# Decoder trunk step: conditions and first conditioning columns reordered, first product group cut into half-depth products

## The chip, the cores and the metric

The kernel runs on one core of a Trainium2 chip. The metric is the device time of one execution in microseconds (us).

## What is computed

A two-layer decoder trunk works on 288 rows (256 of a prompt, 32 of samples) of 2048 features. Only the start of layer 0 matters here:

```python
m = jax.nn.silu(c) @ w + b                 # c: 9 condition rows, w: 2048 x 6144
shift, scale, gate = jnp.split(m[:, None, :], 3, axis=-1)
h = rmsnorm(x, norm_g[layer]) * (1.0 + scale) + shift
... = jnp.split(h @ w_in, idx, axis=-1)    # w_in: 2048 x 7168
```

So no product with `w_in` can start before the shift and the scale of at least some features are there, and these are themselves a product of the condition rows with a 2048-deep matrix of 50 MB per layer.

## The kernel before

Features lie on the partitions in 16 blocks of 128, `k` = 0 to 15. Each product in `w_in` is made three times for precision: the weight is split into a high and a low part (`WHI` by ScalarE in `hi`, L293; `WLO` by VectorE in `lo`, L298), and so is the input (`HH`, `HL`), and `product` issues three matmuls (L304, L307, L308).

**Weights** come in chunks of 512 KB, numbered `i`, into four slots `WRAW[i % 4]`: four blocks `k` deep and 256 columns wide. The load of chunk `i` waits until `lo(i - 4)` has read its slot. A step `i` of the first 48 (`part_products`) has 24 matmuls with one chunk. Steps 0 to 11 multiply blocks 0 to 3, steps 12 to 23 blocks 4 to 7 and so on; VectorE takes each step's partial sum out of PSUM (`part_out`: a copy, L674, in the first group, an addition, L678, in the later ones). Three pairs of PSUM banks take turns, so step `i` waits for the sum of step `i - 3`.

**Conditioning columns** come in units `a` of 4 MB, each 512 columns over the full depth of 2048, in eight loads into the buffer `XR`, which holds one unit. `ada_sum` (L390, 16 matmuls that the trace shows as 32) sums a unit quarter by quarter and frees each quarter (`x_used`); `ada_copy` (ScalarE, L398), `ada_turn` (L403) and `ada_home` (VectorE, L412, L415) bring it into `ADA`. Unit 0 holds the shift of blocks 0 to 3, unit 1 their scale; units 2 and 3 the same for blocks 4 to 7. With both, `scale4` and `modulate4` make the input of four blocks, and `lo_part` (L447) its low part.

**Order.** Each engine runs its own list in order and waits on semaphores in it. SyncE's list holds all these loads: unit 0, chunk 0, unit 1, chunks 1 to 3, unit 2, chunks 4 to 10, unit 3, chunks 11 to 15, unit 4 and so on. A load of unit `a` waits for the sum of unit `a - 1`. The loop of the first 48 steps is, per step `i`:

```python
part_products(pe, i)                       # TensorE; then a sum if i in SUM_AT, a turn if i in TURN_AT
hi(act, i + 4)                             # ScalarE; then ada_copy, modulate4
part_out(dve, i); lo(dve, i + 4)           # VectorE; then ada_home, scale4, lo_part
```

Before the loop, units 0 and 1 are summed and the input rows turned (`x_turn`, L498) on TensorE, in that order of arrival: rows, conditions, unit 0, rows, unit 1. VectorE scales the turned rows (`x_scaled`, L537) and builds a mask (`own_mask`, L579 to L585).

## Time and profile before

| | |
|---|---|
| median of 3 runs | 1283.02 us (1279.35 to 1283.18) |
| the profiled execution, its own time | 1283.61 us |
| its span in the profile | 1281.9 us |
| TensorE busy | 1197.0 us, 93% |
| chain that ended last | TensorE 83% of the span |

The span leaves 1.7 us of the profiled execution's own time outside. TensorE's idle time is what the time can be shortened by, and most of it lies in the first 75 us.

### The profile page before, as it was taken

The numbers are of one execution on the slowest core, as the hardware profiler recorded it, in microseconds if no ns is written. First come the engines' busy times: TensorE is split into PE (matmuls) and PEld (weight loads), VectorE is DVE, ScalarE is ACT, GpSimd is POOL, SyncE is SP. The second block draws the span as 40 slices with busy tenths as digits, with TensorE's granted clock in tenths as the row PEclk, the third lists the DMA queues.
The fourth block names the chain that finished last, engine by engine and source line by source line (L and its number), as shares of the span: only waits on it lengthen the run. The fifth ranks groups of instructions, "written<-read, shape, count | busy, mean of one in ns | idle before, by whom it ended". The sixth has DMA issues, their size and how long they took to land.

```text
span 1281.9 us, 23762 instructions
## 1 busy us (share of the span) xinstructions
PE 1197.0 (93%) x9394; PEld 1064.2 (83%) x9394; DVE 714.5 (56%) x1343; ACT 564.6 (44%) x715; POOL 335.9 (26%) x195
## 2 busy tenths in 40 slices
PE   5799999999999899999999995999999999989995
PEld 2589797978888778788889885999998999989995
DVE  2745556554544546534355446399999993583112
ACT  3323433333343444422243235466666664473442
POOL 1000000000000001000000002565676668486771
PEclk9899999999999999999999998999999999999998
DMA  9999899999887767999999993384766445353432
GB/s 302 329 315 339 279 333 313 379 360 331 295 300 256 270 225 270 300 354 320 348 369 341 309 323 117 97 280 158 254 211 217 154 141 179 101 165 132 163 117 90
DMA packets 236276, 324.89 MB, mean 253 GB/s; under 512 B 12366, under 2 KB 152462, under 8 KB 235246
## 3 DMA queue, kind: packets, MB, share of 16 engines
...
## 4 chain that ended last, share of the span: by engine, by line
PE 83%; DVE 6%; DMA 4%; issue 2%; ACT 2%; SPq 2%; POOL 0%; ACTq 0%; DVEq 0%; POOLq 0%
PE PS L304 21%; PE PS L308 20%; PE PS L307 20%; PE PS L390 6%; PE PS L973 4%; PE PS L1001 3%; PE PS L1210 2%; DMA XR<-in_ada_w 2%; SPq L377 2%; DVE ACTS L1820 1%; DMA WRAW<-in_ab_w_out 1%; DMA ACTS<-in_x_sample 1%; DVE WLO L298 1%; PE PS L403 1%; ACT WHI L293 1%
## 5 line engine op out<-in xcount | busy, mean ns | idle before, releaser
L304 PE MATMUL PS<-HH,WHI 128*128 128x288 f32 x2176 | 665.9, 306 | 32.0 <-DVE HL L447 20.6
L308 PE MATMUL PS<-HH,WLO 128*128 128x288 f32 x2176 | 646.0, 297 | 0.0
L307 PE MATMUL PS<-HL,WHI 128*128 128x288 f32 x2176 | 645.9, 297 | 0.0
L304 PEld LDWEIGHTS PS<-HH,WHI 128*128 128x128 f32 x2176 | 413.1, 190 | 55.0 <-issue 41.7
L293 ACT ACTIVATE WHI<-WRAW 128x1024 fp32r<-128x1024 f32 x272 | 283.9, 1055 | 371.1 <-PE PS L308 320.5
L307 PEld LDWEIGHTS PS<-HL,WHI 128*128 128x128 f32 x2176 | 413.7, 190 | 0.1
L308 PEld LDWEIGHTS PS<-HH,WLO 128*128 128x128 f32 x2176 | 412.9, 190 | 0.0
L298 POOL TENSOR_TENSOR WLO<-WRAW,WHI 128x1024 fp32r<-128x1024 f32 x128 | 308.1, 2424 | 232.6 <-ACT WHI L293 232.6
L298 DVE TENSOR_TENSOR WLO<-WRAW,WHI 128x1024 fp32r<-128x1024 f32 x144 | 175.9, 1224 | 162.9 <-ACT WHI L293 161.6
L1662 DVE SCALAR_TENSOR_TENSOR PS<-ACTS,CWT,PS 128x288 f32<-128x288 f32 x448 | 192.5, 514 | 0.0
L1638 ACT ACTIVATE ACTS<-ACTS 128x1088 f32<-128x1088 f32 x32 | 70.3, 2197 | 61.2 <-DVE ACTS L1660 34.8
L390 PE MATMUL PS<-XR,CT 128*32 128x512 f32 x768 | 89.6, 606 | 4.3 <-DMA XR<-in_ada_w 3.9
L986 DVE COPY ACTS<-PS 128x512 f32<-128x512 f32 x64 | 44.1, 689 | 78.8 <-PE PS L973 78.1
L973 PE MATMUL PS<-IDENT,XR 128*128 128x128 f32 x512 | 77.7, 274 | 5.1 <-DVE ACTS L986 3.5
L984 ACT ACTIVATE ACTS<-PS 128x512 f32<-128x512 f32 x64 | 38.3, 598 | 81.8 <-PE PS L973 79.8
L973 PEld LDWEIGHTS PS<-IDENT,XR 128*128 128x128 f32 x512 | 60.8, 140 | 11.9 <-issue 4.9
L390 PEld LDWEIGHTS PS<-XR,CT 128*32 128x32 f32 x768 | 22.6, 111 | 53.5 <-issue 45.8
L1428 POOL DMA_DIRECT2D ACTS<-in_a_ws x1 | 0.9, 945 | 230.3 <-PE PS L1001 230.3
L430 DVE TENSOR_TENSOR PS<-PS,ADA 128x64 f32<-128x64 f32 x24 | 5.5, 228 | 88.5 <-PE PS L308 88.5
L678 DVE TENSOR_TENSOR ACTS<-PS,ACTS 128x576 f32<-128x576 f32 x36 | 27.2, 756 | 45.3 <-PE PS L308 45.3
L636 POOL IOTA ACTS<- 128x128 f32 x1 | 0.2, 242 | 193.0 <-DVE HL L447 193.0
L1001 PE MATMUL PS<-ACTS 128*32 128x256 f32 x512 | 32.1, 392 | 6.5 <-DVE ACTS L986 3.8
...
## 6 DMA issues: line engine op xcount, KB each, us to landing
XR<-in_ada_w SPq DMA_DIRECT2D x192, 512.0 KB, 8.5
WRAW<-in_ab_w_in SPq DMA_DIRECT2D x112, 512.0 KB, 7.4
WRAW<-in_c_w_in SPq DMA_DIRECT2D x96, 512.0 KB, 3.8
XR<-in_cache_b_k SPq DMA_DIRECT2D x128, 256.0 KB, 5.0
XR<-in_cache_b_v SPq DMA_DIRECT2D x128, 256.0 KB, 5.5
WRAW<-in_ab_w_out SPq DMA_DIRECT2D x32, 512.0 KB, 10.0
WRAW<-in_c_w_out SPq DMA_DIRECT2D x32, 512.0 KB, 3.2
...
```

What stands on the lines that cost most here:

```text
L293: act.activation(WHI[:, i % 4], WRAW[:, i % 4], ACT.Copy).then_inc(w_hi, 1)
L298: eng.tensor_tensor(WLO[:, c], WRAW[:, c], WHI[:, c].bitcast(F32), ALU.subtract).then_inc(w_lo[c], 1)
L304: first = pe.matmul(out, whi, HH[:, k, :], start=start, stop=False)
L307: pe.matmul(out, whi, HL[:, k, :], start=False, stop=False)
L308: return pe.matmul(out, wlo, HH[:, k, :], start=False, stop=stop)
L390: last = pe.matmul(PS[32 * kk:32 * kk + 32, bank, :], CT[:, 4 * c + kk, :], XR[:, c, kk * 512:(kk + 1) * 512], start=c == 0, stop=c == 3)
L973: last = pe.transpose(PS[:, (M2, M3)[g % 2], (2 * h2 + t) * P:(2 * h2 + t + 1) * P], XR[:, c, at:at + P], IDENT[:])
L984: eng.activation(dst, PS[:, M2, :], ACT.Copy).then_inc(kt_a, 1)
L986: eng.tensor_copy(dst, PS[:, M3, :]).then_inc(kt_d, 1)
L1001: last = pe.matmul(PS[32 * j:32 * j + 32, M0, 0:BLOCK], QM[:, j, h, :], KT[:, hh % 2, j, h2, :], start=h == 0, stop=h == HEADS - 1)
L1638: act.activation(EX[:, lo:hi, 0:64], src, ACT.Copy)
L1662: ins = dve.scalar_tensor_tensor(dst, src, tap, dst, ALU.mult, ALU.add)
```

## The change

Condition rows are loaded and turned first, the input rows after them; the rows' transposes lie between the quarters of unit 0's sum. Units 0 and 1 are now shift and scale together, of blocks 0 and 1 (unit 0) and of blocks 2 and 3 (unit 1), 256 columns each. Only unit 0 is summed before the loop; unit 1 after step 3, unit 2 after step 7, unit 3 after step 11. The first twelve chunks are two blocks deep and 512 columns wide, so steps 0 to 5 need blocks 0 and 1 alone and steps 6 to 11 blocks 2 and 3. Each of these steps makes two half steps with a PSUM bank pair each, and `first_out` takes both sums out: for steps 0 to 5 the first by ScalarE and the second by VectorE, for steps 6 to 11 both by VectorE. The low parts of chunks 0 to 3 go to GpSimd. The turning of the convolution's weights (31 small transposes) moves from after step 4 to after step 3.

```diff
 
+            if i < 12:
+                return win_v, 2 * (i // 6), 3072 + 512 * (i % 6)
             if i < 48:
                 return win_v, 4 * (i // 12), 256 * (12 + i % 12)
...
             c, (view, k, col) = i % 4, w_src(i)
             if i >= 4:
                 sp.wait_ge(w_lo[c], i // 4)
-            sp.dma_start(WRAW[:, c], view[:, k:k + 4, col:col + 256]).then_inc(w_raw[c], 16)
+            if i < 12:
+                sp.dma_start(WRAW[:, c].rearrange("p a b -> p (a b)").rearrange("p (k n) -> p k n", k=2),
+                             view[:, k:k + 2, col:col + 512]).then_inc(w_raw[c], 16)
+            else:
+                sp.dma_start(WRAW[:, c], view[:, k:k + 4, col:col + 256]).then_inc(w_raw[c], 16)
...
                 k = 4 * c + 2 * half
+                if a < 2:
+                    t = half
+                    sp.dma_start(XR[:, c].rearrange("p (k t n) -> p k t n", k=4, t=2)[:, :, t],
+                                 ada_v[0, :, 4 * c:4 * c + 4, 2048 * t + 256 * a:2048 * t + 256 * a + 256]).then_inc(x_rdy[c], 16)
+                    continue
...
+            if a < 2:
+                for t in range(2):
+                    dst = ADA[:, 16 * t + 2 * a:16 * t + 2 * a + 2, :]
+                    src = PS[:, M1, 256 * t:256 * t + 256].rearrange("p (m j r) -> p m r j", m=2, j=4)[:, :, 0:NC9, :]
+                    last = dve.tensor_reduce(dst, src, AX.X, ALU.add)
+                last.then_inc(ada_part, 1)
+                dve.wait_ge(ada_part, a + 1)
+                for t in range(2):
...
             ada_copy(act, 0, 0, M0)
             hi(act, 0)
+            hi(act, 1)
+            modulate(act, 0, 2, 1)
             act.wait_ge(xt_tr, KC)
             act.wait_ge(s_setup_pe, 2)
             act.dma_start(CWROW.rearrange("k (w p) -> k w p", p=P),
                           c_conv_w[0].rearrange("w (k p) -> k w p", p=P)).then_inc(s_cw, 16)
-            ada_copy(act, 1, 1, M0)
-            modulate4(act, 0)
-            for i in range(1, 4):
-                hi(act, i)
+            hi(act, 2)
+            hi(act, 3)
...
+            def between(c):
+                if c == 0:
+                    for t in range(3):
+                        pe.wait_ge(s_rows[t], 16)
+                    for k in range(2):
+                        x_turn(pe, k)
+                elif c == 1:
+                    for k in range(2, 6):
+                        x_turn(pe, k)
+                elif c == 2:
+                    pe.wait_ge(s_vec, 8 * 16)
+                    pe.transpose(PS[:, M2, 0:112], VROWS1, IDENT[0:112, 0:112])
+                    pe.transpose(PS[:, M2, 112:208], VROWS2, IDENT[0:96, 0:96]).then_inc(s_setup_pe, 1)
+                    for k in range(6, 11):
+                        x_turn(pe, k)
+
+            ada_sum(pe, 0, 0, M0, between)
             pe.wait_ge(x_diag, 1)
             for t, rows in ((0, P), (1, P), (2, NS * DS)):
                 last = pe.matmul(PS[:, M3, t * P:t * P + rows], ONES[0:rows, :], DIAG[0:rows, t * P:t * P + rows],
                                  start=True, stop=True)
             last.then_inc(x_rb, 1)
-            ada_sum(pe, 1, 1, M0)
-            ada_turn(pe, 1)
+            x_turn(pe, 11)
+            ada_turn(pe, 0)
+            for k in range(12, KC):
+                x_turn(pe, k)
...
         def start_dve(dve):
+            dve.memset(CROW, 0.0).then_inc(s_cz, 1)
+            dve.wait_ge(s_setup_pe, 1)
+            dve.tensor_copy(CT[:], PS[:, M3, :].rearrange("p (k c) -> p k c", c=32)).then_inc(s_setup_cp, 1)
             for k in range(4):
                 x_copy(dve, k)
-            dve.wait_ge(s_setup_pe, 1)
-            dve.tensor_copy(CT[:], PS[:, M3, :].rearrange("p (k c) -> p k c", c=32)).then_inc(s_setup_cp, 1)
...
+            dve.wait_ge(s_setup_cp, 2)
             ada_home(dve, 0)
+            scale(dve, 0, 2, 1, 1)
+            for k in range(12, KC):
+                x_copy(dve, k)
...
+            for k in range(2):
+                lo_part(dve, HF, k, k, k)
...
+            for i in range(4):
+                lo(pool, i)
             pool.wait_ge(s_hl, KC)
...
-        SUM_AT = {3: 2, 8: 3, 13: 4, 19: 5, 25: 6, 31: 7, 37: 8, 41: 9, 45: 10}
-        TURN_AT = {4: 2, 8: 3, 14: 4, 20: 5, 26: 6, 32: 7, 38: 8, 42: 9, 46: 10}
+        SUM_AT = {3: 1, 7: 2, 11: 3, 13: 4, 19: 5, 25: 6, 31: 7, 37: 8, 41: 9, 45: 10}
+        TURN_AT = {4: 1, 8: 2, 11: 3, 14: 4, 20: 5, 26: 6, 32: 7, 38: 8, 42: 9, 46: 10}
...
+        def first_products(pe, i):
+
+            pe.wait_ge(w_lo[i % 4], i // 4 + 1)
+            for half in range(2):
+                h = 2 * i + half
+                if h == 2:
+                    pe.wait_ge(s_seed_cp, 1)
+                if 3 <= h < 15:
+                    pe.wait_ge((acc_pa, acc_pd)[(h - 3) % 2], (h - 3) // 2 + 1)
+                elif h >= 15:
+                    pe.wait_ge(acc_free, h - 14)
+                for kk in range(2):
+                    k = 2 * (i // 6) + kk
+                    if i % 6 == 0:
+                        pe.wait_ge(s_hl, k + 1)
+                    for n in range(2):
+                        last = product(pe, i, 2 * kk + half, n, k, PART_SETS[h % 3], kk == 0, kk == 1)
+            last.then_inc(w_used, 1)
+
+        def first_out(eng, i, half):
+
+            j, banks = 2 * (i % 6) + half, PART_SETS[(2 * i + half) % 3]
+            eng.wait_ge(w_used, i + 1)
+            dst = A(2 * j * R, 2 * R).rearrange("p (c r) -> p c r", r=R)
+            src = PS[:, banks[0]:banks[0] + 2, 0:R]
+            if i < 6 and half == 0:
+                eng.activation(dst, src, ACT.Copy).then_inc(acc_pa, 1)
+            elif i < 6:
+                eng.tensor_copy(dst, src).then_inc(acc_pd, 1)
+            else:
+                eng.wait_ge((acc_pa, acc_pd)[half], i - 5)
+                eng.tensor_tensor(dst, src, dst, ALU.add).then_inc(acc_free, 1)
...
         def qkv_pe(pe):
             for i in range(NQKV):
                 part_products(pe, i)
+                if i == 3:
+                    pe.wait_ge(s_cw, 16)
+                    pe.wait_ge(ada_done, 1)
+                    for w in range(CW):
+                        last = pe.transpose(PS[:, M1, w * KC:(w + 1) * KC], CWROW[:, w * P:(w + 1) * P], IDENT[0:KC, 0:KC])
+                    last.then_inc(s_cwt, 1)
+                if i == 4:
...
                 hi(act, i + 4)
                 if i in SUM_AT:
                     ada_copy(act, SUM_AT[i], SUM_AT[i], M0)
-                if i in (8, 20, 32):
-                    modulate4(act, i // PAIRS_QKV + 1)
+                if i < 6:
+                    first_out(act, i, 0)
+                if i == 4:
+                    modulate(act, 2, 2, 2)
+                if i in (11, 20, 32):
+                    modulate(act, 4 * (i // PAIRS_QKV) + 4, 4, i // PAIRS_QKV + 3)
...
-                part_out(dve, i)
+                if kg:
+                    part_out(dve, i)
+                else:
+                    if i >= 6:
+                        first_out(dve, i, 0)
+                    first_out(dve, i, 1)
                 lo(dve, i + 4)
...
                 if i in TURN_AT:
                     ada_home(dve, TURN_AT[i])
-                    if i in (8, 20, 32):
-                        scale4(dve, kg + 1)
-                if kg < 3 and 9 <= j <= 10:
+                if i == 4:
+                    scale(dve, 2, 2, 2, 2)
+                    for k in (2, 3):
+                        lo_part(dve, HF, k, k, k)
+                if i in (11, 20, 32):
+                    scale(dve, 4 * kg + 4, 4, 2 * kg + 4, kg + 3)
+                if i == 11:
+                    for k in range(4, 8):
+                        lo_part(dve, HF, k, k, k)
...
             load_ada4(sp, 0, 0)
-            w_load(sp, 0)
-            load_ada4(sp, 1, 1)
-            i = 1
-            for a, upto in ((2, 4), (3, 11), (4, 16), (5, 21), (6, 27), (7, 33), (8, 39), (9, 45), (10, 49), (11, 53),
+            i = 0
+            for a, upto in ((1, 4), (2, 8), (3, 12), (4, 16), (5, 21), (6, 27), (7, 33), (8, 39), (9, 45), (10, 49), (11, 53),
```

**SyncE, the loads after unit 0** (`XR` is the buffer of the conditioning units, `WRAW` that of the chunks). Before:

```order
L377 DMA XR<-in_ada_w 128x2x512
L287 DMA WRAW<-in_ab_w_in 128x4x256 [waits w_lo0]
L287 DMA WRAW<-in_ab_w_in 128x4x256 [waits w_lo1]
L287 DMA WRAW<-in_ab_w_in 128x4x256 [waits w_lo2]
L287 DMA WRAW<-in_ab_w_in 128x4x256 [waits w_lo3]
L287 DMA WRAW<-in_ab_w_in 128x4x256 [waits w_lo0]
L287 DMA WRAW<-in_ab_w_in 128x4x256 [waits w_lo1]
L287 DMA WRAW<-in_ab_w_in 128x4x256 [waits w_lo2]
L377 DMA XR<-in_ada_w 128x2x512 [waits x_used0]
```

These are chunks 4 to 10 between the last load of unit 2 and the first of unit 3. Now, between the last load of unit 2 and the first of unit 3:

```order
L390 DMA XR<-in_ada_w 128x2x512
L292 DMA WRAW<-in_ab_w_in 128x2x512 [waits w_lo0]
L292 DMA WRAW<-in_ab_w_in 128x2x512 [waits w_lo1]
L292 DMA WRAW<-in_ab_w_in 128x2x512 [waits w_lo2]
L292 DMA WRAW<-in_ab_w_in 128x2x512 [waits w_lo3]
L390 DMA XR<-in_ada_w 128x2x512 [waits x_used0]
```

Now four chunks, 8 to 11, lie between them; chunk 8 stands behind unit 2 and chunk 12 behind unit 3.

**ScalarE, the loop's steps 3 and 4** (L301 is `hi`, L413 `ada_copy`, L738 `first_out`, L646 and L649 `modulate`). Before, with `hi` at L293 and `ada_copy` at L398:

```order
L293 ACTIVATE WHI<-WRAW 128x1024 [waits w_used,w_raw3]
L398 ACTIVATE SCR<-PS 128x512 [waits ada_turned,x_used3]
L293 ACTIVATE WHI<-WRAW 128x1024 [waits w_used,w_raw0]
L293 ACTIVATE WHI<-WRAW 128x1024 [waits w_used,w_raw1]
L293 ACTIVATE WHI<-WRAW 128x1024 [waits w_used,w_raw2]
```

Now:

```order
L301 ACTIVATE WHI<-WRAW 128x1024 [waits w_used,w_raw3]
L413 ACTIVATE SCR<-PS 128x512 [waits ada_turned,x_used3]
L738 ACTIVATE ACTS<-PS 128x576 [waits w_used]
L301 ACTIVATE WHI<-WRAW 128x1024 [waits w_used,w_raw0]
L738 ACTIVATE ACTS<-PS 128x576 [waits w_used]
L646 ACTIVATE ACTS<-ACTS,ADA 128x256 [waits x_times_factor,scale_ready]
L649 ACTIVATE HH<-ACTS 128x288 [waits rows_normalised,act_chain]
```

ScalarE now takes sums out of PSUM behind each `hi`: the L301 that waits for `w_raw0` is `hi(8)`, and the sum of step 4's first half stands behind it.

**TensorE, from the end of step 3 to step 5** (L762 are the 31 transposes, L403 the sum, L312 opens a product). Now:

```order
L762 MATMUL PS<-IDENT,ACTS 128x16 [waits ada_done,conv_weights_loaded]
L762 MATMUL PS<-IDENT,ACTS 128x16 x30
L403 MATMUL PS<-XR,CT 32x512 [waits x_rdy0,ada_done]
...
L312 MATMUL PS<-HH,WHI 128x288 [waits first_sums_by_dve,w_lo0]
...
L312 MATMUL PS<-HH,WHI 128x288 [waits first_sums_by_act]
...
L312 MATMUL PS<-HH,WHI 128x288 [waits first_sums_by_dve,w_lo1]
...
L312 MATMUL PS<-HH,WHI 128x288 [waits first_sums_by_act]
```

The transposes and a sum of a unit now stand between steps 3 and 4. Every second half step waits for a sum taken out by ScalarE, three half steps earlier.

## Rows read from the trace of the kernel before

**Rows 1.** The page: TensorE's busy tenths in 40 slices; GpSimd's low parts.

```profile
PE   5799999999999899999999995999999999989995
...
L298 POOL TENSOR_TENSOR WLO<-WRAW,WHI 128x1024 fp32r<-128x1024 f32 x128 | 308.1, 2424 | 232.6 <-ACT WHI L293 232.6
```

**Rows 2.** Windows of the front: length, busy us, clock, DMA share, GB/s.

```profile
46.00:58.00 12.00, 11.16 (x72) 10.86 (x72) 9.94 (x19) 5.20 (x9) 0.00 (x0) 0.88 1.07 375
72.00:76.00 4.00, 3.43 (x15) 3.44 (x16) 2.72 (x5) 0.00 (x0) 0.00 (x0) 0.59 1.05 402
80.00:150.00 70.00, 69.14 (x534) 60.46 (x532) 38.41 (x55) 28.27 (x37) 0.00 (x0) 1.00 0.93 316
```

**Rows 3.** Timeline of the first 27 us: start, length, engine, line.

```profile
8.26 1.28 ACT L472 ACT_TABLE_LOAD   x1 [8.26 <-issue]
15.25 3.48 PE L498 MATMUL PS<-IDENT,ACTS 128*128 128x128 f32 x12 [15.25 <-DMA ACTS<-in_x_sample]
18.55 1.89 PE L510 MATMUL PS<-IDENT,ACTS 32*128 32x32 f32 x16
21.22 5.47 PE L390 MATMUL PS<-XR,CT 128*32 128x512 f32 x32 [0.24 <-DVE CT L543]
26.62 6.59 PE L498 MATMUL PS<-IDENT,ACTS 128*128 128x128 f32 x36
```

**Rows 4.** Timeline: `ada_copy` after unit 1's sum, and the first product.

```profile
41.44 0.60 ACT L398 ACTIVATE SCR<-PS 128x512 f32<-128x512 f32 x1 [13.13 <-PE PS L390]
46.05 0.58 PE L304 MATMUL PS<-HH,WHI 128*128 128x288 f32 x1 [2.85 <-DVE HL L447]
```

**Rows 5.** The chain that ended last: the sums of units 4 and 5.

```profile
107.99 3.57 PE PS L390 x32
131.31 3.57 PE PS L390 x32
```

**Rows 6.** Timeline of ScalarE: `hi` of chunks 4, 15, 16 and 27.

```profile
57.90 1.06 ACT L293 ACTIVATE WHI<-WRAW 128x1024 fp32r<-128x1024 f32 x1 [6.74 <-DMA WRAW<-in_ab_w_in]
101.72 1.06 ACT L293 ACTIVATE WHI<-WRAW 128x1024 fp32r<-128x1024 f32 x1 [2.12 <-PE PS L308]
104.90 1.06 ACT L293 ACTIVATE WHI<-WRAW 128x1024 fp32r<-128x1024 f32 x1 [2.12 <-PE PS L308]
148.87 1.06 ACT L293 ACTIVATE WHI<-WRAW 128x1024 fp32r<-128x1024 f32 x1 [1.30 <-DMA WRAW<-in_ab_w_in]
```

**Rows 7.** Timeline of SyncE: unit 6's loads and chunk 27 behind them.

```profile
132.37 4.86 SPq L377 DMA_DIRECT2D XR<-in_ada_w  x8
137.27 0.89 SPq L287 DMA_DIRECT2D WRAW<-in_ab_w_in  x1
```

**Rows 8.** DMA issues to landing: at 60.24, at 137.27, at 136.3 to 137.2 us.

```profile
WRAW<-in_ab_w_in SPq DMA_DIRECT2D x1, 512.0 KB, 3.7
WRAW<-in_ab_w_in SPq DMA_DIRECT2D x1, 512.0 KB, 11.6
XR<-in_ada_w SPq DMA_DIRECT2D x2, 512.0 KB, 9.9
```

**Rows 9.** Groups by line and form, first 250 us: busy, mean ns.

```profile
L298 DVE TENSOR_TENSOR WLO<-WRAW,WHI 128x1024 fp32r<-128x1024 f32 x51 | 62.2, 1223 | 24.1 <-ACT WHI L293 23.9
L293 ACT ACTIVATE WHI<-WRAW 128x1024 fp32r<-128x1024 f32 x51 | 53.5, 1057 | 100.3 <-PE PS L308 84.6 <-DMA WRAW<-in_ab_w_in 15.7
L674 DVE COPY ACTS<-PS 128x576 f32<-128x576 f32 x12 | 9.0, 754 | 6.5 <-PE PS L308 6.5
L537 DVE TENSOR_TENSOR ACTS<-XT,SCR 128x1152 f32<-128x1152 f32 x4 | 5.2, 1353 | 0.0
L691 PE MATMUL PS<-IDENT,ACTS 16*128 16x16 f32 x31 | 2.1, 209 | 0.0
```

**Rows 10.** DMA packets of 124 to 128 us and of 138 to 142 us.

```profile
DMA packets 1318, 1.32 MB, mean 330 GB/s; under 512 B 45, under 2 KB 1317, under 8 KB 1317
DMA packets 822, 1.59 MB, mean 396 GB/s; under 512 B 48, under 2 KB 48, under 8 KB 822
```

More of the change, by code:

```diff
@@ L382, in load_ada4, with ada_sum @@
                 load_ada(sp, x, a, c)
-        def ada_sum(pe, x, a, bank):
+        def ada_sum(pe, x, a, bank, between=None):
             if a:
@@ L392, in ada_sum @@
                 last.then_inc(x_used[c], 1)
+                if between is not None:
+                    between(c)
         def ada_copy(act, x, a, bank):
@@ L503, in start_pe @@
             pe.wait_ge(s_ident, 3)
-            for t in range(3):
-                pe.wait_ge(s_rows[t], 16)
-            for k in range(4):
-                x_turn(pe, k)
             pe.wait_ge(s_silu, 1)
@@ L548, in start_dve @@
             dve.reciprocal(RT[:, 0:3], RT[:, 0:3]).then_inc(s_stat, 1)
-            for k in range(4, KC):
+            for k in range(4, 8):
                 x_copy(dve, k)
@@ L555, in start_dve @@
             last.then_inc(x_diag, 1)
+            dve.wait_ge(s_setup_pe, 2)
+            dve.tensor_copy(VT[:], PS[:, M2, 0:208]).then_inc(s_setup_cp, 1)
+            for k in range(8, 11):
+                x_copy(dve, k)
+            dve.wait_ge(x_rb, 1)
+            link(dve, "dve", dve.tensor_copy(RB, PS[:, M3, 0:R]))
+            dve.wait_ge(xt_cp, 4)
+            x_scaled(dve, 0)
+            x_copy(dve, 11)
+            dve.wait_ge(s_setup_cp, 2)
             ada_home(dve, 0)
+            scale(dve, 0, 2, 1, 1)
+            for k in range(12, KC):
+                x_copy(dve, k)
             dve.wait_ge(s_setup_pe, 3)
             dve.tensor_copy(QROW, PS[:, M2, 0:1])
[L559 to L561 removed]
+            dve.tensor_copy(SLROW, PS[:, M2, 32:33]).then_inc(s_seed_cp, 1)
+            for k in range(2):
+                lo_part(dve, HF, k, k, k)
             dve.wait_ge(xt_cp, KC)
[L563 to L570 removed]
             for kg in range(1, 4):
                 x_scaled(dve, kg)
+            dve.wait_ge(s_seed_cp, 1)
             own_mask(dve)
@@ L686, in qkv_pe @@
                     ada_turn(pe, TURN_AT[i])
-                if i == 4:
-                    pe.wait_ge(s_cw, 16)
-                    pe.wait_ge(acc_free, 3)
-                    for w in range(CW):
-                        last = pe.transpose(PS[:, M3, w * KC:(w + 1) * KC], CWROW[:, w * P:(w + 1) * P], IDENT[0:KC, 0:KC])
-                    last.then_inc(s_cwt, 1)
-                    pe.wait_ge(s_setup_cp, 4)
                 if i >= 45:
```

86 lines of the change are left out of this document (37 added, 49 removed).

## The prediction

> **What bounds the kernel now.** I read the page first: TensorE's slices are full except the first two, the seam at slice 25 and the end [rows 1]. So TensorE bounds the kernel, and any us by which its work stands earlier or later in the front is a us of the total. The windows show that the front ends early: from 80 us on TensorE is busy 69.14 of 70 us at full clock, while DMA moves 316 GB/s of the 396 that it can reach [rows 2, 10], so it has some room. Therefore one number decides: when TensorE begins the sum of unit 4 (after step 13). Before, this is at 107.99 us [rows 5]. From there on the lists of all engines are the same in both kernels, and the next sum follows 23.3 us later [rows 5].
>
> **Work of TensorE up to that sum.** A step of 24 matmuls takes 3.18 us at full clock (104.90 - 101.72) [rows 6], a sum 3.6 [rows 5], the 31 transposes 2.1 [rows 9], a turn 0.6. Before, from the first product at 46.05 [rows 4]: 14 steps 44.5, two sums 7.2, two turns 1.2, transposes 2.1, together 55.0, so 101.1; the other 6.9 us to 107.99 are waits and half clock. The half clock (1.2 of 2.4 GHz) shows at the first product, after a pause of 2.85 us [rows 4], and again after the transposes: 72 matmuls in 11.16 us instead of 9.6, and clock 0.59 in 72 to 76 [rows 2]; each start after a pause costs about 1.5 us.
>
> **Start after the change.** ScalarE's list of loads still holds its table load until about 8.3 + 0.4 us (one more issue ahead of it), and silu ends near 11.9 [rows 3]. The 16 turns of the conditions (1.9) and their copy (0.7) give 14.6, and the first quarter of unit 0's sum (5.47 / 4 = 1.4) ends at 16. The rows came at 15.25 [rows 3]; their first load was issued at 0.8 and now stands behind the zeroing of the condition rows, about 2.4 us later, so I take 18.5 (bounds 17 and 20: only shifted, or slowed by sharing with unit 0 as well). Then TensorE owes 11 row turns (0.87 each slow, 3.48 / 4; 0.55 fast, 6.59 / 12 [rows 3]; five slow, six fast, 7.7), three quarters of the sum (3.6) and the vectors (0.8): unit 0 is summed at 30.6. From there to the first product the new list on VectorE decides: factors 1.0 on TensorE, copy 0.5, scaling 1.35 [rows 9], a row copy 0.5, `ada_home` 0.9, scale and sample rows 1.0, four row copies 2.0, the seeds 0.3, `lo_part` 0.5: 8.0 us, so 38.6. Apart from the scaling these are estimates, small instructions of 0.2 to 0.7 us as the 4.6 us chain from copy to first product holds some ten of [rows 4]. This is 7.4 us earlier than 46.05. Bounds 36 and 40. GpSimd's low parts (2.42 us each [rows 1], twice the 1.22 of VectorE [rows 9]) are ready at 35 and 37.5 for the first two steps and cost nothing there.
>
> **What the new order adds before unit 4's sum.** A third sum and turn, 4.2 us, since unit 1 moves behind the first product. The 12 extra takings out of PSUM are 0.75 us each [rows 9]. On VectorE they fit in a step (2 x 0.75 + 1.22 = 2.7 of 3.18). On ScalarE the half-step sum stands behind `hi`: 1.06 + 0.7 + handshakes = 1.95 against the 1.6 us that TensorE can run on, so 0.35 in each of steps 0 to 2, 1.05 together. So without other waits: 38.6 + 55.0 + 4.2 + 1.05 + 1.5 (half clock at the start) = 100.4, 7.6 us better than before. Step 3 then ends at 54.0 and the sum of unit 1 begins at 56.1.
>
> **First wait: chunk 8 behind unit 2.** Unit 2 can load only as unit 1's sum frees `XR`. The same pattern is measured at unit 6: sum at 131.31, first issue at 132.37, the last load of the unit lands at 147.1 (137.2 + 9.9), and the chunk behind it at 148.9 (137.27 + 11.6), where `hi` waits for it [rows 5 to 8]. Chunk 4 behind unit 2 held `hi` for 6.74 us in the old front as well [rows 6]. So a chunk behind a unit lands 17.5 us after the start of the sum: chunk 8 at 73.6. Before, such a chunk had 7 chunks of lead at unit 3; now every unit up to 3 is followed by the chunk that is needed four steps on. `hi(8)` stands in ScalarE's list ahead of the sum of step 4's first half, and the second half of step 5 needs those banks. With `hi` 1.1, the copy 0.7 and handshakes this half step starts at 56.1 + 19.5 = 75.6; TensorE is there at 56.1 + 3.6 + 3.2 + 0.6 + 1.6 = 65.1. Wait 10.5 us. Behind `hi(8)` VectorE also holds `lo(8)`, `ada_home(1)`, `scale`, and then ScalarE `modulate`: step 6 starts 0.6 us late on its own, a half clock costs 1.5. The end of step 7 comes 10.7 us after this half step: the sum of unit 2 begins at 86.3.
>
> **Second wait: chunk 12 behind unit 3.** It lands at 86.3 + 17.5 = 103.8. Now both sums are VectorE's, and `lo(12)` and `ada_home(2)` stand ahead of the sums of step 9: 103.8 + 1.1 + 1.3 + 0.5 + 0.8 = 107.5 for the second half of step 10. TensorE is there at 86.3 + 12.2 = 98.5 (sum, steps 8 and 9, turn, half a step). Wait 9.0 us and again 1.4 of half clock. Step 11 ends 6.3 us later, 113.8.
>
> **Third wait: blocks 4 to 7.** Before, they were made ready under steps 9 to 11. Now unit 3 is summed right ahead of step 12, and TensorE waits for copy, turn, home, scale, modulate and low part, bounded by what it was before the first product: 4.6 us from 41.44 to 46.05 [rows 4], of which the slow turn was 0.5; I take 4.2, and 0.7 since the four blocks come one by one. 113.8 + 3.6 + 4.2 = 121.6; steps 12 and 13 take 7.1: unit 4's sum begins at 128.7. Its own data, asked for at 114.9, land by 129.7, before its last quarter needs them.
>
> **The sum.** 128.7 - 108.0 = +20.7 us, made against the profiled execution: 1283.6 + 20.7 = 1304.3; the median is 0.6 us lower, so 1303.7.
>
> **Where the price is open.** The lag of 17.5 us counts about twice. Its lower end is a lone chunk's 3.7 us and eight loads at 396 GB/s (8 x 1.32), with the 1.1 to the first issue 15.4 [rows 8, 10]: 4 us less in all. Packets: units 0 and 1 go from 2 KB to 1 KB rows and the first twelve chunks the other way; windows of such packets ran at 330 and 396 GB/s [rows 10], but the first was not short of data. A slow unit 0 (4.2 MB, 2.1 us more) is hidden behind the rows, chunks 0 to 7 land well ahead of use.
>
> The Trainium skill, "DMA: Bandwidth & Descriptors", section "Anatomy of one DMA", fits a DMA from GpSimd's queue to about 2.0 us and its bytes at 436 GB/s. By it the nine loads would take 2.0 + 4.72 / 0.436 = 12.8 us as one stream, where rows 7 and 8 show 16.5; with it each wait would be 3.7 us shorter and the sum 1296. This trace disagrees: these are SyncE's loads, issued as the sum frees quarters.
>
> **Rivals.**
> (a) The forecast: both waits form. 1298 to 1310, chance 0.58.
> (b) The stream is faster than under unit 6, because SyncE's list and the queue are empty when the sum begins. The lag is then between 15.4 and 13.0 (4.72 MB at 396 GB/s and the 1.1 to the first issue [rows 7, 10]); at 14, each wait is 3.5 us smaller: 1303.7 - 7 = 1296.7, chance 0.12. Against it: the issues are paced by the sum's quarters here too. The skill's fit named above would lead to this case.
> (c) Only one wait forms, since chunk 12's lag is taken up by VectorE's margin of one and a half steps: 10.4 us less, 1293, chance 0.08. Against it: the margin is already in the 98.5.
> (d) No wait: loads and chunks overlap so that chunk 8 lands within 7 us of the sum's start (that is the point where it decides), say because the two queues' data arrive in another order. Then 20.7 - 10.5 - 0.6 - 1.5 - 9.0 - 1.4 = -2.3 us: 1281. With the first product at 36 instead of 38.6 this is -5, faster by over 0.3%. For it speaks only the earlier start of 7.4 us; against it 4.7 MB at 396 GB/s. Chance 0.10, of which 0.05 faster.
> (e) More is lost: rows landing at 20, the clock lower for longer after each of three pauses, or chunk 16 behind unit 4 (lands at 131.3, held in VectorE's list ahead of step 14's sum) reaching TensorE: 5 to 10 us more, 1309 to 1314, chance 0.12.
>
> **How the numbers follow.** A measurement tells 0.3% (3.9 us) from no change. Faster is half of (d), 0.05; the same is the other half, 0.05; slower the rest, 0.90. The range 1293 to 1312 leaves out (d) and the ends of (c) and (e), under 0.2; the likeliest case alone has 1298 to 1310.
>
> **What the profile would show.** Right: first product near 38.6; `hi` (L301) waiting some 10 us for DMA near 73 and again near 103; a TensorE wait of about 10 us in the middle of step 5 whose releaser is ScalarE's L738, one of about 9 in step 10 released by VectorE's L743; 4 us ahead of step 12 released by L475; the fourth unit's sum (L403) near 128.7; DMA slices below half near 50 us and 80 us. Wrong: chunk 8 landing before 66 us, or the unit 4 sum before 108.

## The result, and the profile after

| | before | after |
|---|---|---|
| median | 1283.02 us (1279.35 to 1283.18) | 1313.13 us (1309.52 to 1315.33, 4 runs) |
| the profiled execution | 1283.61 us, span 1281.9 | 1309.52 us, span 1307.2 |
| sum of unit 4 starts | 107.99 [rows 5] | 133.52 |

The changed kernel is slower: ratio 1.0239, 95% interval 1.0208 to 1.027, some 30 us. The two profiled executions differ by 25.9 us, and 25.5 of them (133.52 - 107.99) are there when the sum of unit 4 starts. So the front holds the loss, and what comes behind it runs as before.

The page of the changed kernel, TensorE's busy tenths in 40 slices, to be laid beside [rows 1]; the loss is in slices 3 and 4:

```profile
PE   5776999999999899999999988799999999998995
```

Its waits up to 134 us: engine, what it made, line, what it waited for; us in all, times, the longest.

```profile
ACT WHI L301 <- DMA WRAW<-in_ab_w_in: 34.9, 5, 12.9
...
PE PS L312 <- ACT ACTS L738: 9.7, 3, 9.3
...
PE PS L312 <- DVE HL L475: 8.9, 3, 5.9
...
PE PS L312 <- DVE ACTS L743: 8.5, 1, 8.5
...
PE PS L312 <- DVE ACTS L740: 2.2, 1, 2.2
```

Of TensorE's idle time behind the first product 9.3 us are released by `first_out` on ScalarE (L738) and 8.5 by `first_out` on VectorE (L743). Both engines wait in turn for `hi`, and `hi` waits 34.9 us for chunks. The timeline of TensorE places the waits between the sums (start, length, line, and the idle time before with its releaser):

```profile
39.91 0.58 PE L312 MATMUL PS<-HH,WHI 128*128 128x288 f32 x1 [5.87 <-DVE HL L475]
...
50.73 0.37 PE L312 MATMUL PS<-HH,WHI 128*128 128x288 f32 x1 [2.15 <-DVE ACTS L740]
...
59.72 5.34 PE L403 MATMUL PS<-XR,CT 128*32 128x512 f32 x32
...
79.79 0.61 PE L312 MATMUL PS<-HH,WHI 128*128 128x288 f32 x1 [9.32 <-ACT ACTS L738]
...
90.24 3.64 PE L403 MATMUL PS<-XR,CT 128*32 128x512 f32 x32
...
110.96 0.61 PE L312 MATMUL PS<-HH,WHI 128*128 128x288 f32 x1 [8.50 <-DVE ACTS L743]
...
117.74 3.64 PE L403 MATMUL PS<-XR,CT 128*32 128x512 f32 x32
...
125.60 0.58 PE L312 MATMUL PS<-HH,WHI 128*128 128x288 f32 x1 [2.85 <-DVE HL L475]
...
133.52 3.64 PE L403 MATMUL PS<-XR,CT 128*32 128x512 f32 x32
```

And ScalarE's, where `hi` of chunks 8 and 12 waits, to be laid beside [rows 6]:

```profile
78.14 1.06 ACT L301 ACTIVATE WHI<-WRAW 128x1024 fp32r<-128x1024 f32 x1 [11.88 <-DMA WRAW<-in_ab_w_in]
79.10 0.63 ACT L738 ACTIVATE ACTS<-PS 128x576 f32<-128x576 f32 x1
...
107.48 1.06 ACT L301 ACTIVATE WHI<-WRAW 128x1024 fp32r<-128x1024 f32 x1 [12.93 <-DMA WRAW<-in_ab_w_in]
```

Read the two together: unit 1's sum begins at 59.72, chunk 8 can be split at 78.14, 18.4 us later; the copy that stands behind `hi` in ScalarE's list ends at 79.7, and TensorE starts at 79.79. For unit 2 and chunk 12 it is 90.24 and 107.48, 17.2 us. Windows of the time before and inside these stretches (length; busy us of TensorE, its weight loads, VectorE, ScalarE, GpSimd; clock; DMA share; GB/s):

```profile
52.00:60.00 8.00, 7.84 (x76) 7.29 (x78) 5.31 (x6) 2.66 (x3) 0.00 (x0) 1.00 0.01 2
60.00:64.00 4.00, 4.00 (x24) 1.00 (x20) 0.76 (x2) 0.00 (x0) 0.00 (x0) 0.57 0.40 109
72.00:76.00 4.00, 0.00 (x0) 0.00 (x0) 0.00 (x0) 0.00 (x0) 0.00 (x0) 0.76 1.05 398
76.00:80.00 4.00, 0.21 (x1) 0.21 (x2) 0.77 (x1) 1.59 (x2) 0.00 (x0) 0.50 0.92 339
80.00:84.00 4.00, 3.82 (x15) 3.50 (x16) 2.69 (x12) 2.44 (x5) 0.00 (x0) 0.50 0.05 20
84.00:92.00 8.00, 8.00 (x67) 6.64 (x69) 6.04 (x9) 3.15 (x4) 0.00 (x0) 0.98 0.01 2
```

From 52 to 60 and from 84 to 92 us the DMA engines move 2 GB/s: the whole list of loads stands behind a unit whose buffer is in use. Then they run at 398 GB/s while no engine has work, and TensorE starts again at half clock.

### The profile page after: what moved, and what is told of

Same layout as the page of the kernel before. It is cut to its first block, busy times and chain, and to the rows that moved or that the text cites. A ratio compares the mean times of both kernels' runs of the same rounds, so it can differ in the third digit from the quotient of the medians.

```text
span 1307.2 us, 23801 instructions
## 1 busy us (share of the span) xinstructions
PE 1202.7 (92%) x9394; PEld 1067.7 (82%) x9394; DVE 723.5 (55%) x1354; ACT 568.1 (43%) x721; POOL 346.3 (26%) x198
## 3 DMA queue, kind: packets, MB, share of 16 engines
q1 hardware_dynamic: 234064, 312.78, 70.7%
## 4 chain that ended last, share of the span: by engine, by line
PE 81%; DVE 7%; DMA 5%; issue 3%; ACT 2%; SPq 2%; ACTq 0%; DVEq 0%
PE PS L312 20%; PE PS L316 20%; PE PS L315 20%; PE PS L403 6%; PE PS L1065 4%; PE PS L1093 2%; PE PS L1302 2%; SPq L390 2%; DMA WRAW<-in_ab_w_in 2%; DVE ACTS L1912 1%; DMA XR<-in_ada_w 1%; DMA ACTS<-in_x_sample 1%; DMA WRAW<-in_ab_w_out 1%; ACT WHI L301 1%; DVE WLO L306 1%
## 5 line engine op out<-in xcount | busy, mean ns | idle before, releaser
L312 PE MATMUL PS<-HH,WHI 128*128 128x288 f32 x2176 | 668.5, 307 | 55.4 <-DVE HL L475 26.6
L312 PEld LDWEIGHTS PS<-HH,WHI 128*128 128x128 f32 x2176 | 415.0, 191 | 80.3 <-issue 50.6
L301 ACT ACTIVATE WHI<-WRAW 128x1024 fp32r<-128x1024 f32 x272 | 284.0, 1056 | 393.9 <-PE PS L316 304.6
L306 POOL TENSOR_TENSOR WLO<-WRAW,WHI 128x1024 fp32r<-128x1024 f32 x132 | 320.4, 2444 | 262.7 <-ACT WHI L301 262.7
L306 DVE TENSOR_TENSOR WLO<-WRAW,WHI 128x1024 fp32r<-128x1024 f32 x140 | 171.2, 1224 | 183.4 <-ACT WHI L301 182.2
L403 PE MATMUL PS<-XR,CT 128*32 128x512 f32 x768 | 91.6, 615 | 2.5 <-DMA XR<-in_ada_w 1.6
L403 PEld LDWEIGHTS PS<-XR,CT 128*32 128x32 f32 x768 | 22.5, 111 | 49.5 <-issue 44.4
## 6 DMA issues: line engine op xcount, KB each, us to landing
WRAW<-in_ab_w_out SPq DMA_DIRECT2D x32, 512.0 KB, 10.1
```

Of the source, the lines that this page charges most:

```text
L301: act.activation(WHI[:, i % 4], WRAW[:, i % 4], ACT.Copy).then_inc(w_hi, 1)
L306: eng.tensor_tensor(WLO[:, c], WRAW[:, c], WHI[:, c].bitcast(F32), ALU.subtract).then_inc(w_lo[c], 1)
L312: first = pe.matmul(out, whi, HH[:, k, :], start=start, stop=False)
L403: last = pe.matmul(PS[32 * kk:32 * kk + 32, bank, :], CT[:, 4 * c + kk, :], XR[:, c, kk * 512:(kk + 1) * 512], start=c == 0, stop=c == 3)
```

## The experiments

Each was timed beside the kernel before on the same chip, with medians of before between 1281.46 and 1284.14 us. Interval: 95%, of the ratio to before.

| run | median us | ratio | interval |
|---|---|---|---|
| after, a second time | 1314.79 | 1.0242 | 1.0219 to 1.0265 |
| chunks 8 to 11 ahead of unit 2 | 1303.35 | 1.0159 | 1.0142 to 1.0176 |
| chunks 12 to 14 ahead of unit 3 | 1303.87 | 1.0165 | 1.0148 to 1.0182 |
| both | 1293.04 | 1.0087 | 1.0067 to 1.0106 |
| unit 2 summed after step 5 | 1304.71 | 1.0159 | 1.0133 to 1.0184 |
| ScalarE's sums ahead of `hi` | 1313.03 | 1.0245 | 1.0218 to 1.0272 |
| low parts on VectorE | 1311.65 | 1.0223 | 1.0202 to 1.0244 |
| unit 1 summed before the loop | 1294.41 | 1.0089 | 1.0066 to 1.0112 |
| the same, chunks 4, 5 ahead of unit 2 | 1292.11 | 1.0082 | 1.006 to 1.0104 |
| both, units 2 and 3 summed earlier | 1288.74 | 1.0045 | 1.0028 to 1.0062 |
| before, conditions first alone | 1285.14 | 1.0015 | 1.0 to 1.003 |
| reordered | 1280.56 | 1.000 | 0.9983 to 1.0016 |

**The two waits, one at a time.** Only SyncE's list is changed: which chunks are issued ahead of unit `a`.

```diff
-            for a, upto in ((1, 4), (2, 8), (3, 12), (4, 16),
+            for a, upto in ((1, 4), (2, 12), (3, 12), (4, 16),
```

> The changed kernel with one edit: SyncE loads chunks 8 to 11 ahead of unit 2 instead of behind it. Theory (chunk 8's lag behind unit 2 makes the first wait): the 9.3 us wait in step 5 goes, step 6 starts near 73 instead of 83.2 us, the second wait (8.5 us in step 10) stays; the time falls by 9 to 11 us against the changed kernel, to about 1303. Rival (the half steps with their sums behind each hi cost the time, whatever the loads do): less than 3 us.

```diff
-            for a, upto in ((1, 4), (2, 8), (3, 12), (4, 16),
+            for a, upto in ((1, 4), (2, 8), (3, 15), (4, 16),
```

> The changed kernel with one edit: chunks 12 to 14 are loaded ahead of unit 3, chunk 15 behind it. Theory (chunk 12's lag behind unit 3 makes the second wait): the 9.3 us wait in step 5 stays, the 8.5 us wait in step 10 goes, step 12 starts near 115 instead of 125.6; the time falls by 9 to 11 us, to about 1303. Rival (half steps): less than 3 us.

```diff
-            for a, upto in ((1, 4), (2, 8), (3, 12), (4, 16),
+            for a, upto in ((1, 4), (2, 12), (3, 15), (4, 16),
```

> Both edits: chunks 8 to 11 ahead of unit 2 and 12 to 14 ahead of unit 3. Theory: the gains add up, 19 to 22 us, to about 1292; the fourth unit's sum starts near 113 instead of 133.5; what is left above the kernel before is the wait ahead of step 12 and the slow start. Rival (the loads only move the wait to the next unit, since the DMA queue has no room): 10 us or less together.

Each takes its own wait away and leaves the other (8.74 us of the second and 8.39 us of the first). Their steps stand 3 to 6 us later than expected, since their first products begin at 44.7 to 45.2 instead of 39.91. The first is worth 9.8 us (1313.13 - 1303.35), the second 9.3, both together 20.1: they add up, and each is one wait with its half clock behind it. With both gone no wait of TensorE behind the first product is longer than 2.85 us, yet 10.5 us of loss remain (1293.04 against 1282.55). The two waits are two thirds of the loss, not all.

**The lag that starts at a sum.**

```diff
-        SUM_AT = {3: 1, 7: 2, 11: 3,
+        SUM_AT = {3: 1, 5: 2, 11: 3,
-        TURN_AT = {4: 1, 8: 2, 11: 3,
+        TURN_AT = {4: 1, 6: 2, 11: 3,
```

> The sum of unit 2 after step 5 instead of step 7, nothing else; the list of loads stays. Theory (a lag that runs from a unit's sum: chunk 12 stands behind unit 3, whose loads start as unit 2's sum frees the buffer): the sum starts near 83 us instead of 90.24, chunk 12 lands 17.2 us later near 100, the second half of step 10 could start at 83 + 20.7 = 103.7, and TensorE is there at 102.5, so the second wait falls from 8.5 to some 1.2 us and little half clock is left of it: median 1304 to 1307. The first wait stays at 9.3. Rival (the second wait is VectorE's own list, or chunk 12 comes at a time of its own): the wait stays at 8 to 9 us and the time at 1313.

Timelines of TensorE and ScalarE in this kernel:

```profile
87.53 4.19 PE L403 MATMUL PS<-XR,CT 128*32 128x512 f32 x32
...
106.21 1.06 ACT L301 ACTIVATE WHI<-WRAW 128x1024 fp32r<-128x1024 f32 x1 [6.31 <-DMA WRAW<-in_ab_w_in]
...
109.24 0.61 PE L312 MATMUL PS<-HH,WHI 128*128 128x288 f32 x1 [2.54 <-DVE ACTS L743]
```

Here the chunk came 18.7 us after the sum began, and the wait fell from 8.50 to 2.54 us (1.2 was expected, with a lag of 17.2). The time fell by 10.1 us beside the second look at the changed kernel on the same chip (1314.79). The profile shows about half of it: from the first product to the sum of unit 4 this kernel takes 88.2 us and the changed one 93.6. Its profiled execution, 1310.56 us, starts the first product at 44.64 and is the slowest of its five, so where the rest of the 10.1 us lies is not shown. Unit 2's columns are needed much later: their sum is early only because it lets chunk 12 in. The rival, a wait of VectorE's own, falls: TensorE still starts some 3 us behind the split of chunk 12 (3.0 here, 3.5 in the changed kernel).

**Does the order in ScalarE's list matter?**

```diff
+                if i < 6:
+                    first_out(act, i, 0)
                 hi(act, i + 4)
                 if i in SUM_AT:
                     ada_copy(act, SUM_AT[i], SUM_AT[i], M0)
-                if i < 6:
-                    first_out(act, i, 0)
```

> The changed kernel with ScalarE's sums of steps 0 to 5 ahead of hi in its list, so that none of them stands behind a chunk that is late. Theory (the chunk is what all wait for; the input of blocks 2 and 3 stands behind it too, on VectorE and ScalarE): the 9.3 us wait moves from step 5 to the start of step 6 and shrinks by the half step to about 7.7, so the time falls by 1 to 3 us, most of it from the half-step handshakes. Rival (the place of ScalarE's sums makes the wait): the wait goes, and 8 to 10 us with it.

The wait moved by half a step and did not shrink: 10.39 us, where 7.7 were expected and 9.32 were there before this edit; the gain of 1 to 3 us did not come. In this kernel's timeline of TensorE:

```profile
84.31 0.58 PE L312 MATMUL PS<-HH,WHI 128*128 128x288 f32 x1 [10.39 <-DVE HL L475]
```

Now the wait ends with blocks 2 and 3 (`HL`), whose scale on VectorE and modulation on ScalarE still stand behind chunk 8's parts. The late chunk is the cause, and the instruction that passes it on can be exchanged.

**GpSimd's low parts beside VectorE.** `lo` of chunks 0 to 3 is moved from GpSimd's list into VectorE's.

```diff
+            lo(dve, 0)
...
+            for i in range(1, 4):
+                lo(dve, i)
...
-            for i in range(4):
-                lo(pool, i)
```

> The changed kernel with the low parts of chunks 0 to 3 back on VectorE (chunk 0's ahead of the first input's low part, 1 to 3 behind the second's). Theory (a low part on GpSimd stops VectorE's instructions that need the same way into memory): the 2.20 us of the scale's first instruction falls to 0.2, the three scalings from 8.2 us together to about 4.0, the first product starts near 37.8 instead of 39.9, and the time falls by 2 to 4 us. Rival (these instructions are slow for another reason, such as DMA traffic): they stay slow, and 4.9 us more work on VectorE makes the kernel 3 to 6 us slower.

First VectorE and GpSimd in the changed kernel, then VectorE with the low parts moved:

```profile
32.80 0.36 DVE L429 TENSOR_REDUCE ADA<-PS 128x18 f32<-128x72 f32 x2
33.20 1.64 DVE L435 TENSOR_TENSOR ADA<-ADA,VT 128x18 f32<-128x18 f32 x2
34.88 2.20 DVE L634 TENSOR_SCALAR ADA<-ADA 128x18 f32<-128x18 f32 x1
...
40.05 8.27 DVE L574 TENSOR_TENSOR ACTS<-XT,SCR 128x1152 f32<-128x1152 f32 x3
...
31.34 5.70 POOL L306 TENSOR_TENSOR WLO<-WRAW,WHI 128x1024 fp32r<-128x1024 f32 x2 [26.97 <-ACT WHI L301]
40.50 6.59 POOL L306 TENSOR_TENSOR WLO<-WRAW,WHI 128x1024 fp32r<-128x1024 f32 x2 [3.46 <-ACT WHI L301]
```

```profile
36.05 0.27 DVE L435 TENSOR_TENSOR ADA<-ADA,VT 128x18 f32<-128x18 f32 x2
36.35 0.18 DVE L637 TENSOR_SCALAR ADA<-ADA 128x18 f32<-128x18 f32 x1
```

With GpSimd at work a scaling of 18 numbers per partition took 2.20 us; without, 0.18. The two additions ahead of it took 1.64 instead of 0.27. The three scalings of rows took 8.27 instead of 3 x 1.353 [rows 9]. Instructions that read PSUM in the same stretch (L429) kept their length. This is the chain to the first product: from the end of unit 0's sum to the first product it is 10.3 us in the changed kernel (29.65 to 39.91) and 8.0 here (32.50 to 40.50), 3.4 less of blocking and 1.2 more for `lo(0)` in the chain. So the cost on this chain is shown. The Trainium skill, "SBUF — State Buffer", section "SBUF: two separate sides", says that VectorE and GpSimd share a pair of ports under an exclusive lock, held for a whole instruction, which a VectorE instruction with two SBUF inputs, or in a mode that uses two ports, needs; the loser is blocked. These rows agree with it; whether the scaling, which has one such input, ran in such a mode no row shows. The first product itself came at 40.50 and not near 37.8, because TensorE's transposes ran slower in this execution (see below).

Behind the first product the edit costs what it gave. Two rows of it, ScalarE's and TensorE's:

```profile
50.12 1.06 ACT L301 ACTIVATE WHI<-WRAW 128x1024 fp32r<-128x1024 f32 x1 [9.29 <-DMA WRAW<-in_ab_w_in]
...
51.76 0.40 PE L312 MATMUL PS<-HH,WHI 128*128 128x288 f32 x1 [3.81 <-ACT ACTS L739]
```

The wait of 2.15 us ahead of step 2 is gone, and one of 3.81 us stands in the middle of step 1, for the sum that ScalarE takes out behind `hi(4)`. Chunk 4 may load only when `lo(0)` has read its slot: VectorE has done that at 40.0, GpSimd had done it at 34.7. SyncE issues the chunk at 40.02 instead of 34.76, and `hi(4)` starts at 50.12 instead of 45.07. So the low parts on GpSimd also let chunk 4 in early. From the first product to the sum of unit 4 this kernel takes 95.6 us, 2 more than the changed one, and its median gained 1.5 us where 2 to 4 were expected, within the intervals of both. What the blocking alone costs the whole kernel no run shows.

**Unit 1 before the loop.** Unit 1 is summed where it was before, ahead of step 0, and units 2 and 3 after steps 3 and 8, so blocks 2 to 7 are made ready earlier too; the rest of the change stays.

```diff
+            ada_copy(act, 1, 1, M0)
...
+            ada_sum(pe, 1, 1, M0)
...
-        SUM_AT = {3: 1, 7: 2, 11: 3, 13: 4,
+        SUM_AT = {3: 2, 8: 3, 13: 4,
-        TURN_AT = {4: 1, 8: 2, 11: 3, 14: 4,
+        TURN_AT = {0: 1, 4: 2, 8: 3, 14: 4,
...
-            for a, upto in ((1, 4), (2, 8), (3, 12), (4, 16),
+            for a, upto in ((1, 2), (2, 4), (3, 11), (4, 16),
```

> The changed kernel with the sum of unit 1 put back ahead of step 0 (into the 5.9 us in which TensorE idles there), its load ahead of chunks 2 and 3, and units 2 and 3, the chunks behind them and blocks 4 to 7 in the places of the kernel before; conditions first, the half blocks and the half steps stay. Theory (the lost time is the lag of the chunks behind units 2 and 3, the sum ahead of step 12 and the added sum inside the loop): no wait above 3 us after the first product near 40 to 43, the fourth unit's sum starts near 102 to 106, and the kernel runs at 1276 to 1281, faster than before. Rival (the half steps and their sums cost the time themselves): it stays above 1290.

A miss, by 13 us. The timeline of ScalarE, and of TensorE:

```profile
56.97 1.06 ACT L301 ACTIVATE WHI<-WRAW 128x1024 fp32r<-128x1024 f32 x1 [13.00 <-DMA WRAW<-in_ab_w_in]
57.93 0.63 ACT L740 ACTIVATE ACTS<-PS 128x576 f32<-128x576 f32 x1
...
58.62 0.61 PE L312 MATMUL PS<-HH,WHI 128*128 128x288 f32 x1 [12.34 <-ACT ACTS L740]
```

Chunk 4 is now the late one, as it was before the change, where `hi(4)` waited 6.74 us [rows 6] at no cost to TensorE. The difference is what stands behind it. Before, VectorE took the one result of a step out of PSUM, and ScalarE had nothing urgent behind `hi(4)`; now a half-depth step has two results, ScalarE's `first_out(0, 0)` stands behind `hi(4)`, and step 1 waits for its banks. So the half-depth products by themselves take away cover. The next kernel lets chunks 4 and 5 pass (`(2, 6)` in SyncE's list):

> As e5 (measured at 1294.4, with a wait of 12.3 us in step 1 behind chunk 4) with one edit: chunks 4 and 5 are loaded ahead of unit 2, so chunk 6 is the first behind it. Theory (the wait sits wherever the first chunk behind a unit is, since ScalarE's sum of the half step stands behind its hi): the wait of 12.3 us goes from step 1 and comes back two steps later, in step 3, smaller by the two steps, 5 to 7 us; time 1286 to 1290. Rival (the DMA queue is simply full up to 57 us, whatever the order): the wait in step 1 stays at 9 us or more and the time at 1292 or more.

The 12.3 us are gone, but the time missed the 1286 to 1290 expected: the median fell by 2 us, and the ratio to before by 0.07%, less than the intervals can tell. Waits of 3.83 us (VectorE's own mask and scalings, stretched by GpSimd: two scalings took 7.03) and 2.63 us (`hi(6)` waiting for its chunk) took their place.

**What is left without the two waits.** To the kernel with both groups of chunks first are added sums after steps 6 and 10, and chunk 14 goes back behind unit 3 (`(3, 14)` in SyncE's list):

```diff
-        SUM_AT = {3: 1, 7: 2, 11: 3,
+        SUM_AT = {3: 1, 6: 2, 10: 3,
-        TURN_AT = {4: 1, 8: 2, 11: 3,
+        TURN_AT = {4: 1, 7: 2, 10: 3,
...
-                if i in (11, 20, 32):
+                if i in (10, 20, 32):
```

> As e3 (chunks ahead of units 2 and 3, measured at 1293), and units 2 and 3 summed after steps 6 and 10, so that blocks 4 to 7 are made ready under step 11. Theory (the wait ahead of step 12 costs 0.7 and 2.9 us and the slow start behind it 1.5): 2 to 5 us below e3, 1288 to 1291. Rival (unit 3's data or chunk 14 come too late for step 10's end, and the wait only changes its releaser): as e3 or slower.

Its median gained 4.3 us of the 10.5. The wait ahead of step 12 is gone. The profile shows little of the gain: the first product begins at 46.03 and the sum of unit 4 70.7 us later, against 71.7 without this edit, and the profiled execution, 1292.46 us, is the second slowest of eight.

**The conditions alone.** The kernel before, with only `start_act`'s loads and `start_pe`'s transposes exchanged:

```diff
-            act.dma_start(XROW[0], xp_v[0:P]).then_inc(s_rows[0], 16)
             act.wait_ge(s_cz, 1)
             act.dma_start(CROW[0:1, :], c_prompt).then_inc(s_crow, 16)
             act.dma_start(CROW[1:NC9, :], c_sample).then_inc(s_crow, 16)
+            act.dma_start(XROW[0], xp_v[0:P]).then_inc(s_rows[0], 16)
```

> The kernel before with one part of the change alone: the condition rows are zeroed by VectorE, loaded and turned ahead of the input rows; units, chunks, steps and sums as before. Theory (the condition rows are not what the front waits for: unit 1's data are): within 3 us of the kernel before, since the later first load of the rows (2.4 us) and the earlier conditions (3 us) meet in the same sum. Rival (the conditions' place is a gain or a loss of its own): 4 us or more either way.

The interval runs from no difference to 0.3% slower. So this part of the change by itself brings no gain, and it is not what costs 30 us.

**Everything mended together.** Chunks 4 to 8 ahead of unit 2 and 11 to 13 ahead of unit 3; sums after steps 0, 6 and 10; ScalarE's sums and `modulate(2, 2)` ahead of `hi`; `lo` 0 to 3 on VectorE; three of the four `x_scaled` inside the loop.

```diff
-        SUM_AT = {3: 1, 7: 2, 11: 3,
+        SUM_AT = {0: 1, 6: 2, 10: 3,
...
-            for a, upto in ((1, 4), (2, 8), (3, 12), (4, 16),
+            for a, upto in ((1, 2), (2, 9), (3, 14), (4, 16),
...
-            for kg in range(1, 4):
-                x_scaled(dve, kg)
...
+                if i in (13, 15):
+                    x_scaled(dve, (i - 9) // 2)
```

> A version of the changed kernel built from the findings so far: chunks 4 to 8 ahead of unit 2 and 11 to 13 ahead of unit 3; units 1, 2 and 3 summed after steps 0, 6 and 10; ScalarE's sums and the input of blocks 2 and 3 ahead of hi; the low parts of chunks 0 to 3 on VectorE; the scaling of blocks 4 to 15 moved into the loop. Theory (late chunks, GpSimd's low parts, and the sum ahead of step 12 are all that made the change slow): no wait above 2 us after the first product near 38 to 41, the fourth unit's sum near 103 to 107, the kernel at 1278 to 1283, so as fast as before or up to 0.4% faster. Rival (the half steps themselves cost 5 us or more, or the extra sum of unit 1 inside the loop eats the early start): 1287 or more.

All waits of TensorE from 40 to 103 us in it:

```profile
PE PS L312 <- DVE HL L475: 3.6, 1, 3.6
PE PS L418 <- ACT SCR L413: 0.7, 1, 0.7
```

The 3.6 us lie ahead of the first product, at 40.40; behind it TensorE does not wait over 0.7 us. Its profile has unit 4's sum at 102.68, 5.3 us ahead of before, but over 12 and 17 runs the medians are the same (1280.56 and 1281.46). So the change's idea, an earlier first product, can be had without its loss, and is then worth at most 2 us (lower end of the interval: 0.17%). The edits were made together, so what each of them gives is not shown.

**The changed kernel a second time.**

> The changed kernel itself, unchanged, for a second profile and more times. Open is why the medians lie 30.1 us apart and the two profiles only 25.9. Theory A (spread of one execution): the waits of 9.3 and 8.5 us and the sum of unit 4 near 133 us stay within 2 us in the second profile, its own time lies anywhere from 1309 to 1316, the median at 1312 to 1314, and what differs lies ahead of the first product, where the clock rises. Theory B (a loss behind the front that the first profile did not have): the second profile has its fourth sum at 133 to 134 as well but a span of 1311 or more, so 3 to 4 us lost behind it.

The profile repeats: waits of 9.3 and 8.6 us, the sum of unit 4 at 134.16, span 1307.7. Its own time, 1309.9, is again the lowest of its runs (up to 1316.54). Both profiles of it start the first product early, at 39.91 and 40.55; six others whose lists are the same up to there start at 42.6 to 46.0. Rows of the turns and factors, the changed kernel first and then the one with unit 2 after step 5:

```profile
22.26 2.49 PE L526 MATMUL PS<-IDENT,ACTS 128*128 128x128 f32 x12
25.92 2.73 PE L526 MATMUL PS<-IDENT,ACTS 128*128 128x128 f32 x15
29.58 1.05 PE L557 MATMUL PS<-ACTS,ONES 128*128 128x128 f32 x6
```

```profile
22.12 3.51 PE L526 MATMUL PS<-IDENT,ACTS 128*128 128x128 f32 x12
27.82 4.32 PE L526 MATMUL PS<-IDENT,ACTS 128*128 128x128 f32 x15
33.94 1.79 PE L557 MATMUL PS<-ACTS,ONES 128*128 128x128 f32 x6
```

The same instructions took up to 1.7 times as long until about 41 us. An execution of this kind would put the changed kernel at 1309.5 + 4.7 = 1314.2 us, where most of its other runs lie. That fits the missing 4 us between medians and profiles, but those runs have no profile, so it is argued and not shown. Both profiles of the changed kernel are of the early kind, so it is not even shown that this kernel has executions of the other. For it speaks the kernel with chunks 8 to 11 first: its profiled execution, with the late first product (45.20), took 1307.03 us and its three others 1302.80 to 1303.49.

## Why the prediction was right and wrong

Direction and mechanism were right; the time, 1313.13, was 9.4 us above the forecast of 1303.7 and 1.1 us above the range. Of the 9.4 us, 5.2 are there in the profiled execution (1309.52 against the 1304.3 forecast for it), 4.8 of them ahead of unit 4's sum; 3.6 are what the median lies above that execution, and 0.6 what the prediction took off for the median. Since the start of the first product varies from run to run, the step times are best taken as stretches. By the timeline of the changed kernel:

| stretch | forecast us | measured us |
|---|---|---|
| up to the first product | 38.6 | 39.9 |
| first product to unit 1's sum | 17.5 | 19.8 |
| to the half step behind wait 1 | 19.5 | 20.1 |
| to unit 2's sum | 10.7 | 10.4 |
| to the half step behind wait 2 | 21.2 | 20.7 |
| to the end of step 11 | 6.3 | 6.8 |
| to step 12 | 7.8 | 7.9 |
| to unit 4's sum | 7.1 | 7.9 |
| sum | 128.7 | 133.5 |

**Right.** Both waits, their places and their releasers: 10.5 and 9.0 us forecast, 9.32 and 8.50 measured; `hi` waiting for DMA; DMA idle from 52 to 60 and again from 84 to 92 us. The lag of 17.5 us, read from unit 6 before, was 18.4 and 17.2. That the first came so near is in part luck: it is 17.5 to 18.4 us only where unit 1's sum ran at half clock (5.34 us), and 15.8 and 16.0 in the two kernels where this sum took 3.64 and chunk 8 was late (low parts on VectorE; ScalarE's sums first). A slow sum frees the buffer later, and the prediction had it at 3.6. The stretch of 10.7 us behind the first wait is 0.6 more than the terms named for it (1.6, 0.6, 1.5 and 6.4). Rival (b), a faster stream, falls with it, and so do (c) and (d). Unit 4's sum behind it and the later lists behaved as they did before.

**Wrong: "ready at 35 and 37.5 for the first two steps and cost nothing there".** That was the step that failed. GpSimd's low parts were on time, and they held up VectorE's scale and additions by 3.4 us on the chain to the first product, and its row scalings by 4.2 us behind it. The forecast of the first product missed by only 1.3 us by luck: unit 0's sum ended 0.9 us early (29.65 against 30.6), and without the blocking the chain would have taken 6.9 us instead of the 8.0 forecast. To the 4.2 us belongs the wait of 2.15 us ahead of step 2, which no step of the prediction had: `first_out` L740 stands behind the scalings and the mask, and 4.2 us earlier it would have been done before TensorE came (worked out from these rows; no run shows it alone). That list could hold TensorE before the change too, behind the same scalings and mask:

```profile
58.93 0.40 PE L304 MATMUL PS<-HH,WHI 128*128 128x288 f32 x1 [1.72 <-DVE ACTS L674]
```

This step's cost lies in the first two stretches of the table, together 3.6 us longer than forecast. The low parts themselves were seen before the change at 2424 ns [rows 1]; what was not asked was which instructions of VectorE lay beside them now.

**Wrong in size: "each start after a pause costs about 1.5 us".** The sum held three such starts, 4.4 us in all. Lengths of the same work at either level, from the changed kernel's timeline: the first 36 matmuls took 6.4 us instead of 4.8; unit 1's sum, behind the small transposes, 5.34 instead of 3.64; the half step behind wait 1 3.2 instead of 1.6, and steps 6 and 7 another 0.7; the last one and a half steps behind wait 2 6.8 instead of 4.8; steps 12 and 13 7.9 instead of 6.4. In all 9.1 us. Not all of it shows in the time: the 1.7 us of the slow sum lie ahead of wait 1 and go into it, and part of the rest cancels against the 1.05 us for ScalarE's takings in steps 0 to 2, which showed only 0.25.

**The price without waits.** The prediction had 23.0 us for the two waits with what hangs on them and -2.3 for the rest; the runs have 20.1 and +10.5 (the kernel with both groups of chunks first). So the waits were priced 3 us too high, and all that rival (d) stood on, 1281 us without waits, was 12 too low. From first product to unit 4's sum, the stretch took 61.9 us before (46.05 to 107.99), 93.6 after, and 71.7 with both waits gone (44.72 to 116.44), where the prediction's terms give 67.1: third sum and turn 4.2, then the wait ahead of step 2, the one ahead of step 12 (2.85 and 0.72) and the half clock. The earlier start pays for this with 6 us in the profile of the changed kernel and with 1.3 in that one.

**The range.** Rival (e) named "the clock lower for longer after each of three pauses" and reached to 1314; it is the one nearest the result. The range cut it off at 1312. The start of the first product was bounded by 36 and 40 us; the profiles show 39.9 to 46.0.

**Open.** Whether the other runs of the changed kernel really lose their 2 to 7 us ahead of the first product, and why TensorE's early transposes take long in some executions.
